# A two-layer block on one Trainium2 core: the opening's columns rebuilt, and stretch and maximum of the attention logits in one VectorE operation

## The reference

```python
cond = jax.nn.silu(c)                                  # (1, 1024)
mod = cond @ ada_w + ada_b                             # (1, 6144), six parts of 1024
sh_m, sc_m, gt_m, sh_f, sc_f, gt_f = split(mod, 6)
h = rms_norm(x, norm_mix_g) * (1.0 + sc_m) + sh_m
proj = h @ w_in                                        # all mixers' inputs and gates
...
scores = q @ k.T * 64 ** -0.5 - slope[h] * abs(t - s)  # 4 heads, 2 maps, blocks of 128 queries
p = softmax(scores)                                    # slope[h] = 2 ** (-2 * (h + 1))
w = p[0] - lam * p[1]
```

## Time and profile before

| | |
|---|---|
| median of 3 executions | 2429.36 us (2426.98 to 2429.91) |
| the profiled execution | 2430.64 us, of which the span of the trace is 2428.9 us |
| PE busy | 2301.2 us (95% of the span) |
| DVE, ACT, POOL busy | 1190.7, 1013.0, 1057.2 us |
| transfers | 240 MB, mean 99 GB/s |

### The profile page before, as it was taken

One profiled execution on the slowest core, in us unless ns is written; L12 is line 12 of the kernel. 1 busy time (PEld: TensorE's weight loads), 2 busy tenths in 40 slices (PEclk: granted clock), 3 DMA queues, 4 the chain that ended last, 5 costly groups with the idle time before them and its releaser, 6 DMA issues. The chain is left out here.

```text
span 2428.9 us, 30245 instructions
## 1 busy us (share of the span) xinstructions
PE 2301.2 (95%) x12206; PEld 1951.0 (80%) x12206; DVE 1190.7 (49%) x1806; ACT 1013.0 (42%) x1902; POOL 1057.2 (44%) x806
## 2 busy tenths in 40 slices
PE   4889989899999999999999999999999999999997
PEld 4668767678788888888888888889978888888887
DVE  4476778774452221447576243451154345734254
ACT  2586564555353332455463222263333234522223
POOL 2344333334454444642345444444444434544443
PEclk9899999899999999999999999999999999999999
DMA  5312223336312222221112222222222222222321
GB/s 225 111 50 72 105 89 115 122 127 233 147 70 104 101 90 105 87 96 36 70 70 89 102 87 104 104 83 92 88 87 87 91 83 87 87 104 83 109 92 65
DMA packets 42507, 239.86 MB, mean 99 GB/s; under 512 B 4992, under 2 KB 7040, under 8 KB 17152
## 3 DMA queue, kind: packets, MB, share of 16 engines
q1 hardware_dynamic: 39312, 231.23, 25.6%
q10 hardware_dynamic: 3056, 6.70, 0.9%
HBM read 226.38 MB, written 8.39 MB: 97 GB/s over the span
## 5 line engine op out<-in xcount | busy, mean ns | idle before, releaser
L2407 POOL TENSOR_TENSOR WL<-RAW,WH 128x512 fp32r<-128x512 f32 (+1 forms) x724 | 956.6, 1350 | 1211.9 <-ACT WH L1207 1200.3
L697 PE MATMUL PS<-HHI,WH 128*128 128x512 f32 (+1 forms) x1688 | 660.0, 391 | 19.8 <-DVE HLO L1758 9.3
L697 PE MATMUL PS<-HLO,WH 128*128 128x512 f32 (+1 forms) x1688 | 641.9, 380 | 0.0
L697 PE MATMUL PS<-HHI,WL 128*128 128x512 f32 (+1 forms) x1688 | 641.6, 380 | 0.0
L1207 ACT ACTIVATE WH<-RAW 128x512 fp32r<-128x512 f32 (+1 forms) x724 | 398.8, 612 | 385.9 <-PE PS L697 353.8
L697 PEld LDWEIGHTS PS<-HHI,WH 128*128 128x128 f32 x1688 | 321.1, 190 | 100.2 <-issue 21.7
L697 PEld LDWEIGHTS PS<-HHI,WL 128*128 128x128 f32 x1688 | 320.7, 190 | 60.9
L697 PEld LDWEIGHTS PS<-HLO,WH 128*128 128x128 f32 x1688 | 321.1, 190 | 56.7 <-issue 1.7
L697 PE MATMUL PS<-UF,WH 128*128 128x512 f32 (+1 forms) x832 | 224.0, 357 | 0.0
L1752 DVE TENSOR_TENSOR T<-PS,R 128x512 f32<-128x512 f32 x112 | 76.9, 689 | 215.4 <-PE PS L697 204.8
L697 PEld LDWEIGHTS PS<-UF,WH 128*128 128x128 f32 x832 | 148.3, 189 | 22.7
(11 more groups left out here) (326 smaller groups left out, 3391.4 us busy)
## 6 DMA issues: line engine op xcount, KB each, us to landing
RAW<-in_wts SPq DMA_DIRECT2D x192, 1024.0 KB, 4.8
spill<-T SPq DMA_DIRECT2D x24, 256.0 KB, 2.9
RAW<-in_wts SPq DMA_DIRECT2D x8, 768.0 KB, 4.3
GT<-spill SPq DMA_DIRECT2D x20, 256.0 KB, 4.6
FW<-in_wts SPq DMA_DIRECT2D x4, 1024.0 KB, 15.3
X<-in_xt SPq DMA_DIRECT2D x1, 2048.0 KB, 16.4
out_x<-X SPq DMA_DIRECT2D x16, 128.0 KB, 1.7
X<-in_xt SPq DMA_DIRECT2D x2, 768.0 KB, 8.8
```

The lines of the kernel that those rows point to most:

```text
L697: return e.matmul(o_, l, r, start=start, stop=stop)
L2407: return e.tensor_tensor(o_, a, b, f)
```

## The change

**The opening.** The eight units are cut anew and come in another order (`EARLY`): the scale in four units of 4 row blocks by 512 columns ("g", group, half), the shift in four as before ("s"). All eight have a place of their own; x comes in two halves right behind the first unit; `c` has its own small transfer ahead of `V`. The unit for `cqk` comes fifth of the units behind x. The squares are four operations of 128x1024, each with its own tile `SQP`; PE adds all eight tiles (`mm(MEAN, ones, ...)`), and ACT's Ln and Exp work in place in PSUM. DVE sums only the scale, in 128x512 operations into PSUM, per group of four columns. The shift is made by PE with `CC` as the stationary operand, as one row of 256 numbers (`share`); ACT copies the row (`row_out`), and PE turns it to the partitions (`turn_row`). A column waits for the scale of its group of four (`am`) and the shift of its pair (`shift_out`) instead of all sixteen numbers. POOL no longer scales columns. It keeps the low parts of columns 2, 3 and 5, between the pieces of `cqk`.

**The attention.** The queries are evicted from PSUM times -`LEAN[h]` (2^(2h-1)), so that the new operation can form (PSUM + distance) * (-1/LEAN) and the row maximum of the result together. One small operation then serves both maps. The first map's operation now waits for the Exp of both maps of the block before.

**Small moves.** The mask cast stands two steps later on DVE, and `LWT` and `MF` lie elsewhere, so their transfers start earlier.

```diff
+EARLY = [("g", 0, 0), ("s", 0), ("g", 0, 1), ("s", 1), ("s", 2), ("g", 1, 0), ("g", 1, 1), ("s", 3)]
...
+    for what, n, *half in EARLY:
+        if what == "g":
+            cols("ada_w", "ada", [(4 * half[0], 4)], [(1024 + 512 * n, 512)])
+        else:
+            cols("ada_w", "ada", full, [(256 * n, 256)])
...
+    LEAN = [2.0 ** (2 * h - 1) for h in range(4)]
...
+        load(0)
+        for n in range(2):
+            e.dma_start(X1[:, 4 * n:4 * n + 4, :], xin[:, 4 * n:4 * n + 4, :]).then_inc(*up(f"x{n}", ("x_in", n), by=16))
+        for i in (1, 2, 3, 4, 8, 5, 6, 7, 9):
             load(i)
         done = 9
...
+        def share(n):
+
+            i, b = early("s", n), 3 + n % 2
+            free(b)
+            q.wait_ge(*at(("raw", i)))
+            for k in range(8):
+                t = mm(PS[0:1, b, 0:256], CC[:, k:k + 1], first[i][:, 256 * k:256 * k + 256], k == 0, k == 7)
+            t.then_inc(*up("psum", ("row", n), ("raw_free", i)))
+
+        def turn_row(n):
+
+            b = 3 + n % 2
+            q.wait_ge(*at(("row_out", n)))
+            for m in range(2):
+                t = mm(PS[:, b, 256 + m:257 + m], ROW[n % 2][:, 128 * m:128 * m + 128], ones[0:1, 0:1], True, True)
+            t.then_inc(*up("psum", ("shifts", n)))
+            holds(b, ("shift_out", n))
+
+        def gains(g):
...
+            q.wait_ge(*at(("acc", g, 7)))
+            for m in range(4):
+                t = mm(PS[:, 5 + g, m:m + 1], DD[0][:, g, 128 * m:128 * m + 128], ones[:, 0:1], True, True)
+            t.then_inc(*up("psum", ("gain", g)))
+            holds(5 + g, ("gain_out", g))
+
+        def qk_rows(*ks):
+            i = U["cqk", 0]
+            for k in ks:
+                for m in range(2):
+                    t = rows(BANK[i, m], i, 128 * m, [k], [H[k]], [("h", "mix", k)], k == 0, k == 7)
+                    if k == 7:
+                        full(t, i, m)
+
+        q.wait_ge(*at(("vec",)))
+        for p in range(4):
+            q.wait_ge(*at(("sqp", "mix", p)))
+            for c in range(2):
+                t = mm(MEAN, ones, SQP[p][:, c, :], p + c == 0, p + c == 4)
+        t.then_inc(*up("psum", ("sum", "mix")))
+        holds(7, ("sc", "mix", 7))
         q.wait_ge(*at(("cc",)))
-        for a in FOLD:
-            if a == 6:
-                sums("mix")
-            r = first[a] if a < 6 else RAW[a % 2]
-            q.wait_ge(*at(("raw", a)))
...
-            holds(b, ("mod_out", 7))
-
-        tiles_wide(U["cqk", 0], H, hk("mix"))
+        share(0)
+        gains(0)
+        turn_row(0)
+        share(1)
+        turn_row(1)
+        share(2)
+        qk_rows(0)
+        turn_row(2)
+        qk_rows(1, 2, 3)
+        gains(1)
+        share(3)
+        qk_rows(4)
+        turn_row(3)
+        qk_rows(5, 6, 7)
         tiles(U["lr", 0], H, hk("mix"), 0)
...
+        def column(k):
+
+            tm = T0[k % 4][:, :]
+            q.wait_ge(*at(("sc", "mix", k)))
+            q.wait_ge(*at(("shift_out", k // 2)))
+            e.activation(tm, tm, ACT.Identity, bias=shift["mix"](k)).then_inc(*up("a_norm", ("scs", "mix", k)))
+            q.wait_ge(*at(("scs", "mix", k)))
+            e.activation(HHI[:, k, :], tm, ACT.Copy).then_inc(*up("h_hi", ("h_hi", "mix", k)))
+
+        def row_out(n):
+            q.wait_ge(*at(("row", n)))
+            if n > 1:
+                q.wait_ge(*at(("shifts", n - 2)))
+            e.activation(ROW[n % 2], PS[0:1, 3 + n % 2, 0:256], ACT.Copy).then_inc(*up("a_norm", ("row_out", n)))
...
+        c0, cn = VOFF["c"]
+        e.dma_start(CC[:, :], vec[:, c0:c0 + cn]).then_inc(*up("c", ("c_in",), by=16))
...
-        rstd("mix")
+        q.wait_ge(*at(("c_in",)))
+        e.activation(CC[:, :], CC[:, :], ACT.Silu).then_inc(*up("a_norm", ("cc",)))
         for p in range(4):
-            split(U["cqk", 0], p)
-        norm_mix()
-        q.wait_ge(*at(("h", "mix", 7)))
+            q.wait_ge(*at(("x_in", p // 2)))
+            e.activation(SQP[p][:, :, :], X1[:, 2 * p:2 * p + 2, :], ACT.Square).then_inc(*up("a_norm", ("sqp", "mix", p)))
+        table()
+        q.wait_ge(*at(("sum", "mix")))
+        e.activation(MEAN, MEAN, ACT.Ln, scale=1.0 / 1024, bias=EPSC[:, 0:1]).then_inc(*up("a_norm", ("ln", "mix")))
+        q.wait_ge(*at(("ln", "mix")))
+        e.activation(MEAN, MEAN, ACT.Exp, scale=-0.5).then_inc(*up("a_norm", ("r", "mix")))
+        i = U["cqk", 0]
+        row_out(0)
+        column(0)
+        column(1)
+        row_out(1)
+        split(i, 0)
+        split(i, 1)
+        column(2)
+        row_out(2)
+        column(3)
+        split(i, 2)
+        split(i, 3)
         e.dma_start(LWT[:, :], mixc[:, NM:NM + LW]).then_inc(*up("lw", ("lw",), by=16))
         e.dma_start(MC[:, :], mixc[:, 0:NM]).then_inc(*up("mixc", ("mixc",), by=16))
         e.dma_start(MF[:, :], masks).then_inc(*up("masks", ("masks",), by=16))
-
-        i = U["cqk", 0]
+        column(4)
+        column(5)
+        row_out(3)
         split_after(i)
+        column(6)
+        column(7)
         for m in range(2):
             q.wait_ge(*at(("t", i, m)))
             q.wait_ge(*at(("h", "mix", 4 + m)))
...
+        def gains(g, half):
+
+            i = early("g", g, half)
+            if half == 0 and g == 0:
+                q.wait_ge(*at(("cc",)))
+            q.wait_ge(*at(("raw", i)))
+            ac = PS[:, 5 + g, :]
+            for kk in range(4):
+                k, w_ = 4 * half + kk, first[i][:, 512 * kk:512 * kk + 512]
+                if k == 0:
+                    t = ts(ac, w_, CC[:, 0:1], None, MUL)
+                else:
+                    q.wait_ge(*at(("acc", g, k - 1)))
+                    t = stt(DD[0][:, g, :] if k == 7 else ac, w_, CC[:, k:k + 1], ac, MUL, ADD)
+                t.then_inc(*up("d_mix", ("acc", g, k), *([("raw_free", i)] if kk == 3 else [])))
+
+        def gain_out(g):
+            q.wait_ge(*at(("gain", g)))
+            q.wait_ge(*at(("vec",)))
+            cs = slice(8 + 4 * g, 12 + 4 * g)
+            tt(MOD[:, cs], PS[:, 5 + g, 0:4], v("ada_b", 8 + 4 * g, 4), ADD).then_inc(*up("d_mix", ("gain_out", g)))
+            q.wait_ge(*at(("gain_out", g)))
+            stt(AM[:, 4 * g:4 * g + 4], MOD[:, cs], 1.0, v("gmix", 4 * g, 4), ADD, MUL).then_inc(*up("d_mix", ("am", g)))
+
+        def shift_out(n):
+            q.wait_ge(*at(("shifts", n)))
+            q.wait_ge(*at(("vec",)))
+            tt(MOD[:, 2 * n:2 * n + 2], PS[:, 3 + n % 2, 256:258], v("ada_b", 2 * n, 2), ADD).then_inc(*up("d_mix", ("shift_out", n)))
+
+        def scaled(k):
+            q.wait_ge(*at(("r", "mix")))
+            q.wait_ge(*at(("am", k // 4)))
+            if k > 3:
+                q.wait_ge(*at(("h", "mix", k - 4)))
+            stt(T0[k % 4][:, :], X1[:, k, :], gain["mix"](k), MEAN, MUL, MUL).then_inc(*up("d_norm", ("sc", "mix", k)))
+
+        def column(k):
+            q.wait_ge(*at(("h_hi", "mix", k)))
+            tt(HLO[:, k, :], T0[k % 4][:, :], HHI[:, k, :].bitcast(F32), SUB).then_inc(*up("h_lo_d", ("h", "mix", k)))
...
+        gains(0, 0)
+        gains(0, 1)
+        gain_out(0)
+        scaled(0)
+        shift_out(0)
+        for k in (1, 2, 3):
+            scaled(k)
+        column(0)
+        shift_out(1)
+        column(1)
+        gains(1, 0)
+        shift_out(2)
+        gains(1, 1)
+        gain_out(1)
+        scaled(4)
+        scaled(5)
+        column(4)
+        shift_out(3)
+        scaled(6)
+        scaled(7)
+        column(6)
+        column(7)
         i = U["lr", 0]
...
                         q.wait_ge(*at(("weights", ph, pq) if i else ("attn_t", ph, pq)))
+                        q.wait_ge(*at(("p", ph, pq, 1)))
                     d_ = DIST[:, 384 - 128 * qb:896 - 128 * qb]
-                    stt(SB[i][:, :], d_, -8.0 * slope, PS[:, i, :], MUL, ADD).then_inc(*up("d_ev", ("logits_ev", h, qb, i)))
-                    q.wait_ge(*at(("logits_ev", h, qb, i)))
-                    if h or qb:
-                        q.wait_ge(*at(("p", ph, pq, i)))
-                    e.reduce_max(SC[:, 20 + i:21 + i], SB[i][:, :], AX).then_inc(*up("d_mix", ("max", h, qb, i)))
-                    q.wait_ge(*at(("max", h, qb, i)))
-                    ts(SC[:, 22 + i:23 + i], SC[:, 20 + i:21 + i], -0.125, None, MUL).then_inc(*up("d_mix", ("top", h, qb, i)))
+                    e.tensor_tensor_reduce(SB[i][:, :], PS[:, i, :], d_, -1.0 / LEAN[h], -1e38, ADD, MAX,
+                                           SC[:, 20 + i:21 + i]).then_inc(*up("d_ev", ("logits_ev", h, qb, i)))
+                q.wait_ge(*at(("logits_ev", h, qb, 1)))
+                ts(SC[:, 22:24], SC[:, 20:22], -0.125, None, MUL).then_inc(*up("d_mix", ("top", h, qb)))
...
+                ts(QK[:, 2 * n + m, 0, :], ps, -LEAN[2 * n + m], None, MUL).then_inc(*up("d_ev", ("ev", i, m)))
...
-        add_squares("mix")
-        for p in range(4):
-            split(U["cqk", 0], p)
-        norm_mix()
+        split(U["cqk", 0], 0)
+        column(2)
```

(5 more changed lines are left out.)

161 lines of the change are left out of this document (19 added, 142 removed).

## The result

The changed kernel takes **2385.0 us** (median of 4, 2384.5 to 2388.0) against 2429.6 us before, a ratio of 0.982 (95% interval 0.980 to 0.984), thus 40 to 48 us faster. The sign, the two gaining parts and the order of events were right; the gain was nearly half as large again (44.6 us for 31).

What follows compares the result with a forecast made beforehand. PE bounds the kernel, idle mainly in the opening (set by the modulation vector) and in attention (late DVE and ACT queues). 2430.64 - 24 (opening) - 7 (attention) = 2399.6 us profiled, median 2398, range 2386 to 2416.

Steps and rivals of the forecast that it cites:

- The opening, 24 us: Opening up to first eviction: last column 22 us sooner, 1.6 from transfers issued ahead of it, 0.4 behind.
- What follows: From last column through first eviction and small transfers: eviction gap 2.7 to 1.1 us, chain unchanged, 0.4 us added.
- The attention, 7 us: Attention blocks: fused stretch and maximum saves 1.3 us of DVE per block; 7 us gained, between 0 and 14.
- Of 21 us only what PE waited for comes back: Attention: of DVE's 21 us, `SCT` waits give at most 8.5 us, ACT waits some 3, others 2 at most.
- Some of the lower clock goes with them: Attention: with PE's shorter waits some time at the lower clock goes too; no size of its own.
- the sign: Attention on DVE: 1.7 to 1.8 us per block from first ISA to the small operation's end.
- the wait for both Exps: Attention: new wait for both Exps of the block before costs nothing, since weights needing both are already awaited.
- Behind: From 560 us' counterpart on: stages keep equal lengths.
- The shares ran at the upper clock: Opening, rival 1 claimed the opposite: shares keep PE at the lower clock, 8 us each; 2412 us, chance 17%.
- half pace: Attention, rival 2's second case: operation at half pace, 3.05 us per block, no gain; 2405 us, rival's chance 11%.
- a dear operation: Attention, rival 3: the new ISA operation costs far more; at 3.5 us each 2446, slower than before, chance 4%.
- x landed where it was forecast: Opening: x halves land at 9.3 and 11.8 us; rival 4 had no sooner than 19.3, 2402 us, chance 5%.

Runs made afterwards that it cites:

- attention's part alone: Kernel before with only the one-operation form for stretch and maximum and the scaled eviction of the queries: 2410.2 us, ratio to before 0.993.
- e3: Changed kernel plus two DVE maxima over a constant per attention block, behind the small operation that releases Exp: 2393.4 us, ratio to before 0.986.
- e5: Changed kernel with the one operation taking the minimum, read by Exp as its bias, and the small operation dropped: 2377.4 us, ratio to before 0.979.

## Why the prediction was right in its parts and missed the size

- **The opening, 24 us.** 24.0 at the first eviction. Arrival (9.5 and 12.0, forecast 9.3 and 11.8), sums (9.1 us, 10), 1/rms (22.4, 23.2), shares (3.6, 4) and last column (50.1, 50 to 51) came as worked out. For the sums two errors offset in part: five of the sixteen instructions ran at the lower level, two and a half products instead of two, but a product took 1.7 and 0.86 us instead of 1.9 and 1.05. The first product was 2 us sooner, as the shares were. The first eviction follows the last column by 1.2 us (1.1). DVE's scalings, with 1/rms in PSUM, took 0.69 to 0.75 us, also beside POOL (45.98), where they had 0.91 before.
- **What follows.** "Its 16 small transfers, the next pieces and the whole chain behind keep their lengths", with 0.4 added: wrong by 2.2 us. I gave the small transfers' neighbours a price without reading when the next unit goes out; it was issued among them, and now goes out ahead.
- **Up to the attention stage** 2.0 us came that I had nowhere. Two of the 16 blocks lie there, and the repeated trace of the changed kernel shows 0.3 instead of 2.0, so it is partly chance.
- **The attention, 7 us.** This is the step that failed. "Of 21 us only what PE waited for comes back" was about right for the idle time: 8.2 us in the stage, `SCT` by 5.5 and `SS` by 2.9. "Some of the lower clock goes with them" got no number of its own, so it stands in the sum of 7 at nothing. It is 6.2 us of busy time here and 10.5 with the attention's part alone, and it is most of the 7.4 us that were missing. The duration of the operation was right (1.71 us per block by its parts, 1.75 forecast; from start to end it is 1.50, for the 1.7 to 1.8 named as the sign, since the overlap was left out).
- Within that step the reason was off as well. I priced DVE's 21 us of work and called the wait for both Exps and the sooner Exp small change ("about 0.5 us sooner"). The runs show the order ahead of Exp as the larger share: 9.3 us of the stage for 1.27 us per block.
- **Behind**, equal lengths were forecast; 3.1 us came, and the repeats show that as chance.
- The sum: 4.6 us more than forecast up to 290 us, 7.4 more in the attention stage, 3.1 of chance: 15.1 of the profiled execution. The median, with less luck in it, gained 44.6 us.
- **Rivals.** The shares ran at the upper clock (3.61 us each, not 8). The operation ran at full pace, so neither half pace nor a dear operation came about; the Trainium skill's rule of half pace (Vector Engine (DVE) Microarchitecture Reference, Points that are easy to get wrong) did not bite with one source in PSUM, as its letter has it; no run here has such an operation with both in SBUF. x landed where it was forecast.

With the clock counted as high as the idle time, the attention would have been 14 us and the sum 2391; a range shifted by the same 7 us would have held the result.

## What to carry to other kernels

Where PE waits often and shortly in a stage whose granted clock is below 1, count a removed wait nearly twice, as an estimate: here each microsecond of idle time took 0.7 to 1.3 us of busy time along (e3, e5, the changed kernel and the attention alone, against before). Ask of every helper operation not only how long it is but who is released behind it: moving 1.3 us of DVE work from ahead of Exp to behind it was worth 9 us over 14 blocks, and letting it go 0.2 us of work and one map earlier 8 us. In an opening that is one chain on PE, a late input is paid in full to its end.

## What the runs showed of the hardware

- The one operation (out = (a + b) x constant, and its extreme, a in PSUM, b in SBUF) takes 0.68 us for 128x512, as a plain stretch does, and its readout 0.08 us; maximum and minimum alike.
- Products of 256 columns with a one-column stationary operand left PE at the upper clock: a share of sixteen instructions took 3.61 us, four times alike, thus 0.23 us each, half of the 0.43 us from one 512-column instruction of the sum to the next once at the upper level. The pace is what shows it: the profile's granted clock reads 1.00 all through the first 60 us, also from 10 to 15 us, where the sum's instructions came every 0.86 us.
- Two operations of the attention with SBUF operands alone vary in duration by a factor of two to three. Instructions on `SB`, 262 to 300 us of the changed kernel (ns min/median/max):

```profile
L1781 DVE TENSOR_SCALAR SB<-SB,SC x3: 545/546/1573, 262.6 to 294.6; 128x512 f32<-128x512 f32 x3
L1784 DVE SCALAR_TENSOR_TENSOR SB<-SB,SC,SB x3: 750/1640/1648, 263.1 to 295.2; 128x512 f32<-128x512 f32 x3
L2103 DVE CUSTOM_DVE_ANT_0 SB<-PS,MC x4: 676/678/679, 275.6 to 291.8; 128x512 f32<-128x512 f32 x4
```

  The third, with one operand in PSUM, took 0.67 to 0.69 us in all 28 cases of the stage. The Trainium skill (SBUF — State Buffer, Who interferes with whom) names two kinds of DVE instructions as held up by GpSimd: those with two SBUF inputs, and those in a two-port mode. The second operation is of the first kind; whether the first one ran in a two-port mode no row shows, and no experiment tried whether POOL is what slowed them.
- The first transfer of the changed kernel on ACT's queue, 4 KB for `CC`, beside 0.5 MB of `V` and the first units, took 5.2 us to land:

```profile
CC<-in_vec ACTq DMA_DIRECT2D x1, 4.0 KB, 5.2
```

- How much of a stage is granted the lower clock is not fixed by its waits alone: with the same products and 27 to 28 us idle, the granted clock was 0.95 and 0.96 in the two runs of the changed kernel, and 0.98 and 0.97 in the two of the attention alone.
